# Reversing the column order of the projections with stationary weights in a two-layer decoder trunk

## The reference, cut to what matters

```python
for i in range(DEPTH):
    h = _rmsnorm(x, attn_norm_g[i])
    if i % 2 == 0:
        mix = _stick_breaking_attention(h, sb_w_qkv[0], sb_w_o[0])
    else:
        mix = _dsa_attention(h, dsa_w_in[0], ...)
    x = x + mix
    h = _rmsnorm(x, ffn_norm_g[i])
    x = x + _conv_ffn(h, ffn_w_up[i], ffn_conv_w[i], ffn_conv_b[i], ffn_w_down[i])
```

## Time and profile before

| | us |
|---|---|
| median of the two timed runs | 2218.64 |
| the two runs | 2217.64 and 2219.65 |
| profiled execution, span from first to last instruction | 2216.0 |
| what lies around the span (median less span) | 2.64 |
| matmuls busy in the profiled execution | 2209.4 |

### The profile page before, as it was taken

One profiled execution on the slowest core, in us unless ns is written; L12 is line 12 of the kernel. 1 busy time (PEld: TensorE's weight loads), 2 busy tenths in 40 slices (PEclk: granted clock), 3 DMA queues, 4 the chain that ended last, 5 costly groups with the idle time before them and its releaser, 6 DMA issues.

```text
span 2216.0 us, 34772 instructions
## 1 busy us (share of the span) xinstructions
PE 2209.4 (100%) x12470; PEld 1935.2 (87%) x12470; DVE 1484.4 (67%) x1753; ACT 1177.3 (53%) x1409; POOL 14.3 (1%) x21
## 2 busy tenths in 40 slices
PE   9999999999999999999999999999999999999999
PEld 8888898888888888888899888888888888888887
DVE  7666556677777777555578888667777777774443
ACT  7565555555555555444455466555555555553333
POOL 0000000000000000000010000000000000000000
PEclk9999999999999999999999999999999999999999
DMA  7555555555555555565566544555555656566664
GB/s 270 166 168 177 171 162 181 195 185 190 189 193 186 189 190 191 190 190 189 191 212 198 177 157 139 161 183 191 182 198 181 194 184 198 180 193 201 201 199 136
DMA packets 113829, 411.55 MB, mean 186 GB/s; under 512 B 12769, under 2 KB 13537, under 8 KB 113761
## 3 DMA queue, kind: packets, MB, share of 16 engines
q1 hardware_dynamic: 112320, 406.70, 56.5%
q10 hardware_dynamic: 1008, 2.30, 0.3%
q0 software_dynamic: 432, 1.57, 0.2%
HBM read 408.42 MB, written 2.10 MB: 185 GB/s over the span
## 4 chain that ended last, share of the span: by engine, by line
PE 99%; DMA 0%; SPq 0%; DVE 0%; ACT 0%; issue 0%; DVEq 0%
PE psum L1301 99%; DMA raw<-w_all 0%; PE psum L1621 0%; PE psum L1557 0%; DVE w_lo L747 0%; ACT w_hi L289 0%; SPq L237 0%; SPq L235 0%; DVE upad L822 0%; SPq L236 0%; SPq L234 0%; DVEq L83 0%
## 5 line engine op out<-in xcount | busy, mean ns | idle before, releaser
L747 DVE TENSOR_TENSOR w_lo<-raw,w_hi 128x1024 fp32r<-128x1024 f32 x769 | 935.6, 1224 | 678.6 <-ACT w_hi L289 672.8
L1301 PE MATMUL psum<-xg,w_hi 128*128 128x512 f32 (+1 forms) x3936 | 1358.3, 392 | 1.9 <-DVE w_lo L747 1.0
L289 ACT CAST w_hi<-raw 128x1024 fp32r<-128x1024 f32 x770 | 803.1, 1049 | 771.4 <-PE psum L1301 767.6
L1301 PE MATMUL psum<-xg,w_lo 128*128 128x256 f32 (+1 forms) x3920 | 1090.8, 278 | 0.0
L1301 PEld LDWEIGHTS psum<-xg,w_hi 128*128 128x128 f32 x3936 | 736.0, 187 | 156.7 <-issue 2.2
L1301 PEld LDWEIGHTS psum<-xg,w_lo 128*128 128x128 f32 x3920 | 742.6, 189 | 2.6 <-issue 2.2
L1301 PE MATMUL psum<-hid,w_hi 128*128 128x512 f32 x704 | 244.1, 391 | 0.0
L1301 PE MATMUL psum<-w_hi,hid 128*128 128x512 f32 x704 | 217.9, 390 | 0.0
L1301 PE MATMUL psum<-hid,w_lo 128*128 128x256 f32 x704 | 197.4, 280 | 0.0
L1301 PE MATMUL psum<-att,w_hi 128*128 128x512 f32 x512 | 178.8, 393 | 0.0
L1301 PEld LDWEIGHTS psum<-hid,w_hi 128*128 128x128 f32 x704 | 131.7, 187 | 28.6
(11 more groups left out here) (176 smaller groups left out, 1062.9 us busy)
## 6 DMA issues: line engine op xcount, KB each, us to landing
raw<-w_all SPq DMA_DIRECT2D x770, 512.0 KB, 3.8
xres<-x_in SPq DMA_DIRECT2D x3, 512.0 KB, 9.0
cst<-consts_in ACTq DMA_DIRECT2D x2, 768.0 KB, 6.6
raw<-w_all SPq DMA_DIRECT2D x2, 256.0 KB, 3.6
xres<-x_in SPq DMA_DIRECT2D x2, 256.0 KB, 3.8
out_t<-part POOLq DMA_DIRECT2D x1, 512.0 KB, 7.3
out_t<-conv POOLq DMA_DIRECT2D x1, 512.0 KB, 7.4
out_t<-gates POOLq DMA_DIRECT2D x1, 512.0 KB, 7.0
```

The lines of the kernel that those rows point to most:

```text
L289: act.copy(w_hi[:, c % RING, :], raw[:, c % RING, :]).then_inc(hi_ready, 1)
L747: dve.tensor_tensor(w_lo[:, c % RING, :], raw[:, c % RING, :], f32(w_hi[:, c % RING, :]), ALU.subtract).then_inc(lo_ready, 1)
L1301: return pe.matmul(o, lhsT, rhs, start=start, stop=True, skip_group_check=True)
```

## The change

A new local function `back` takes an access pattern, goes to the last element of its last dimension and reads that dimension with step -1. `proj` wraps the output and the moving operand of both matmuls in it. Column n of the activations still goes to column n of the bank; the order in which the columns pass is reversed. The stationary operands are unchanged, and the other functions that issue matmuls are unchanged.

```diff
+            def back(ap):
+
+                n = ap.shape[-1]
+                end = ap[..., n - 1:n]
+                return bass.AP(end.tensor, end.offset, [*ap.ap[:-1], [-1, n]])
+
             def proj(c, i, per, bank0, act_in, kts, k0_, cols, first, by_tile=False, upper_free=None):
...
-                        mm(psum[:, bank0 + ct, :], w_hi[:, s, w], act_in[:, k, :], first and kk == 0)
-                        last = mm(psum[:, bank0 + ct, 0:T], w_lo[:, s, w], act_in[:, k, 0:T])
+                        mm(back(psum[:, bank0 + ct, :]), w_hi[:, s, w], back(act_in[:, k, :]), first and kk == 0)
+                        last = mm(back(psum[:, bank0 + ct, 0:T]), w_lo[:, s, w], back(act_in[:, k, 0:T]))
                 last.then_inc(piece_used, 1)
```

## The result

The changed kernel takes 2247.71 us (two runs, 2247.65 and 2247.77) against 2218.64: a ratio of 1.0133, 95% interval 1.0104 to 1.0163, 29 us more. The forecast was no change, 2218.6 with an own range of 2205 to 2235. The time is inside the wide range of 2200 to 3790, but that range was so wide for the sake of rival 1, which didn't happen, and the forecast case didn't happen either: the loss is small and clear.

The account below looks back on a forecast made before the run. TensorE's back-to-back matmuls were taken to bound the kernel. The profiled span 2216.0 plus three terms of 0 (instructions, dependences, access rate) and 2.6 us around it gave 2218.6 us, range 2200 to 3790.

Parts of the forecast that it names:

- rival 1: All 4880 pairs: every column takes two periods, 0.299 to 0.319 us more a pair, time taken as 3730; chance 0.22.
- the forecast case: Whole kernel: no change, 2218.6 us, own range 2205 to 2235; chance 0.60, including the compiler turning both patterns around again.
- The bound: Whole kernel: TensorE's matmuls, busy 2209.4 of 2216.0 us and 99% of the chain, set the time.
- the count of 4880 pairs: Projection with stationary weights: 3664 pairs on xg, 704 on hid, 512 on att, 9760 of 12470 matmuls.
- First, instructions: Edited projection: no instruction added, removed or moved, reversed patterns built before the program runs; cost nothing.
- Second, dependences: PSUM writes of a pair: shortest distance between writes to one column stays 256 columns, 106 ns; cost nothing.
- The third term: Edited matmuls: rate of step -1 reads from SBUF and writes to PSUM, bounded by 2087 and two periods a column; taken as zero.
- the reading of the gap: Between matmuls: a fixed 13 to 14 ns each, 0.027 us a pair, independent of column order.
- The analogy from the two-run pattern: Index projection's 16 matmuls of 384 columns, two runs of 192, show plain 0.415 ns a column, so reversal should cost nothing.
- Rival 2: Each of 9760 reversed matmuls starts later by a fixed 0.0135 us: 132 us, time 2350; chance 0.10 with other sizes.
- Rival 3: Edited pairs: the fixed gaps between matmuls go away, time 2087; chance 0.05.
- The sign "more than 9 ns": Edited pairs: prediction is wrong if high-to-high distance moves by more than 9 ns (44 us / 4880).

Follow-up runs that it names:

- high only: Changed kernel with only the 512-column matmul of each pair reversed, reading and writing, the 256-column one ascending: ratio 1.014 to the kernel before, pair 353.3 ns.
- low only: Changed kernel with only the 256-column matmul of each pair reversed, the 512-column one ascending: ratio 1.0135 to the kernel before, pair 353.3 ns.
- the moved kernel: Both weight buffers placed 64 bytes further on by pads: kernel before 1.0144 (2250.23 us), changed kernel 1.0099 (2240.17 us).

## Why the prediction was wrong, step by step

- The bound, the count of 4880 pairs and the distance of 345 to 347 ns held, and every nanosecond on a pair showed in full: 29.9 us by pairs, 29.8 in the span. That nothing can hide it was right.
- "First, instructions" and "Second, dependences" held: nothing was added, and writes in the reversed order alone cost nothing (1.0002).
- The third term failed: "The value I take is zero". It measured 6.67 ns a pair on 4032 pairs and about half of that on the rest, 29 us.
- The step beneath it that failed is the reading of the gap: "it belongs to each matmul and not to the order of its columns". I fitted two rows, 512 and 384 columns, and took the 0.027 us of a pair for two constants. The runs show a gap that goes by where the activations and the weights lie to each other in SBUF, by direction, length and what ran before: from 48 periods (64 weight columns) to 96 (a low matmul of 384 columns) for a plain pair, not always 64. The trace of before already held the sign. In the attention stage of layer 0, whose pairs are at 350 on average, runs of 15 to 46 of the same plain pair, from the same line, take (94.83 - 93.77) / 3 = 0.353 us:

```profile
93.77 0.40 PE L1301 MATMUL psum<-xg,w_hi 128*128 128x512 f32 x1
...
94.12 0.40 PE L1301 MATMUL psum<-xg,w_hi 128*128 128x512 f32 x1
...
94.48 0.40 PE L1301 MATMUL psum<-xg,w_hi 128*128 128x512 f32 x1
...
94.83 0.40 PE L1301 MATMUL psum<-xg,w_hi 128*128 128x512 f32 x1
```

  Had I laid this beside the earlier trace rows, a constant gap would have been out, and +6.7 ns a pair, 4032 x 6.67 = 27 us, would have been a possible term with a row of its own.
- The analogy from the two-run pattern was sound as far as it went (two runs or blocks of 128 cost nothing), but didn't bear on a gap that isn't in the pattern.
- Rival 1, half the rate, didn't happen; the streaming rate of one column per period stayed. Only step 2 halved it.
- Rival 2, a start cost of 0.0135 us on each matmul, had the right sign, and its smaller sizes took in the 29 us, but its price was 4.6 times too large (132 us) and its mechanism wrong: the way from the high start to the low one grew by 8.3 ns (230.0 to 238.3) and that from low to high fell by 1.7 (116.7 to 115.0), where it said the same for both; the cost isn't per reversed matmul (high only = low only = both) and turns into a gain at another place. Rival 3, faster, was dismissed because "the rows deny" a gap that depends on order; the moved kernel shows that it does, in both directions.
- The sign "more than 9 ns" from high to high didn't come: 6.67 ns is less. It was taken from a resolution of 2%, and the runs told 1.3% from no change.
- Two smaller readings were off and bear on nothing: 376 in 130 us counts matmuls that the window cuts, so the pair is 346.7 ns and not 345.7, and around a profiled span lie 1.85 us (2247.65 less 2245.8), not 2.6.

Not settled: what in SBUF or in TensorE's two reads makes the gap, why it moves in steps of 8 and 16 periods, and why a pair pays once where the last stage pays each time. The runs show that relative place, direction, length and the number of weight columns set it; that the reads of activations and weights collide is an argument, not a measurement. A stationary side read in the other direction wasn't tried.

## What to carry to other kernels

When one engine runs back to back, the distance from start to start is the quantity, and its part that isn't streaming should be read in every stage before it is called a constant; two lengths for the same instruction in one trace say that something beside it matters. A change of access order, and any new buffer that moves others, can shift such a stream by 1 to 2% without adding an instruction, so a small loss or gain should be tested with a pad before it is put down to the edit. Compare each stage, since one placement helped one stage and hurt another.

## What the runs showed of the hardware that I had not expected

- A pair of matmuls of 512 and 256 columns, each read in one run of step 1 or -1, took 340.0 to 353.4 ns at the same granted clock (1.000), by placement, direction and number of weight columns; moving the weights by 64 bytes cost 1.4% of the kernel.
- The dependence repeats within 512 bytes of relative place: activations +112 columns gave the lengths of weights +16 (353.3 plain, 351.1 reversed).
- The same plain pair on the same buffers has two steady lengths: 346.7 ns over 70 pairs and 353.1 over 22 in one stage of the kernel before. A stage of 704 pairs held 346.7 throughout in one kernel and, with its activations 512 bytes further on, 353.3 in another.
- A moving read of 256 columns with step 2 took 215 ns from start to start instead of 117.
- Fewer stationary columns shortened a plain pair at 64 (340.0) but not at 32 (348.3).
- Writing PSUM from the last column to the first cost nothing.
